# Picking rounds and modulation sums placed beside single attention jobs, the output product's wait split in four, and a square taken before the last output unit

## The reference

```python
mod = c_silu @ w_ada + b_ada                     # 1024 x 3072: the modulation
shift, scale, gate = split(mod, 3)
u = rms_norm(x, norm_g) * (1 + scale) + shift
z = u @ w_in                                     # 1024 x 8772, split by columns
# A: indexed attention: a query sees its top 64 keys by score
score = einsum('bth,bths->bts', iw * w_scale, relu(einsum('bthd,bsd->bths', iq, ik)))
top_val, top_idx = top_k(where(causal, score, -inf), 64)
# B: window attention with sinks; C: stick-breaking attention
merged = sigmoid(ma)*(ya @ w_br_a) + sigmoid(mb)*(yb @ w_br_b) + sigmoid(mc)*(yc @ w_br_c)
x = x + gate * (merged @ w_out)
```

## Time and profile before

| | |
|---|---|
| time, median of three runs | 1428.66 us |
| the profiled execution's own time | 1429.06 us |
| its span, first to last instruction | 1427.3 us |
| PE busy | 1371.8 us, 96% |
| DVE busy | 662.4 us, 46% |
| ACT busy | 419.9 us, 29% |
| POOL busy | 167.2 us, 12% |
| read from HBM | 222.62 MB, 157 GB/s over the span |

### The profile page before, as it was taken

The page is one execution under the profiler, slowest core; times in us unless marked ns, Lnnn a source line. Parts: engine busy times, 40 slices in busy tenths (PEclk is TensorE's granted clock), DMA queues, the critical chain, the costliest instruction groups (busy, mean ns, idle before and its releaser), DMA issues.

```text
span 1427.3 us, 19283 instructions
## 1 busy us (share of the span) xinstructions
PE 1371.8 (96%) x7590; PEld 1127.4 (79%) x7590; DVE 662.4 (46%) x1458; ACT 419.9 (29%) x773; POOL 167.2 (12%) x191
## 2 busy tenths in 40 slices
PE   6989999999998999999999999999999999999996
PEld 4878888888776888888888878877777788887764
DVE  1475334554238644324245331245493532467466
ACT  2312222311020222334322312342344422433442
POOL 0202200000011030000021100013140000243000
PEclk9999999999998999999999999999999999999999
DMA  9645555565433544444333332446322334432230
GB/s 385 248 154 209 209 177 206 188 252 224 176 135 136 211 155 177 148 160 148 121 142 120 118 118 98 151 169 225 126 89 92 116 128 146 168 119 89 89 148 30
DMA packets 31915, 224.93 MB, mean 158 GB/s; under 512 B 3920, under 2 KB 4048, under 8 KB 5072
## 3 DMA queue, kind: packets, MB, share of 16 engines
q1 hardware_dynamic: 31824, 223.68, 42.6%
HBM read 222.62 MB, written 1.05 MB: 157 GB/s over the span
## 4 chain that ended last, share of the span: by engine, by line
PE 85%; DVE 10%; issue 2%; ACT 2%; POOL 1%; DMA 0%; DVEq 0%; SPq 0%; ACTq 0%; POOLq 0%
PE event L1003 42%; PE event L994 9%; PE event L1147 5%; PE event L1213 5%; PE logits L1079 3%; PE mixed_out L1135 3%; PE turns L1098 3%; PE event L1240 2%; PE event L1172 1%; PE event L1177 1%; PE logits L970 1%; DVE region L1734 1%; PE event L1313 1%; DVE region L2200 1%; PE event L982 1%
## 5 line engine op out<-in xcount | busy, mean ns | idle before, releaser
L1003 PE MATMUL event<-u,ring 128*128 128x256 f32 x3072 | 685.2, 382 | 4.8 <-ACT u L1350 2.4
L1003 PEld LDWEIGHTS event<-u,ring 128*128 128x128 f32 x3072 | 578.7, 191 | 97.8 <-issue 18.6
L994 PE MATMUL event<-ring,u 128*128 128x256 f32 (+1 forms) x704 | 152.0, 373 | 0.0
L994 PEld LDWEIGHTS event<-ring,u 128*128 128x128 f32 x704 | 128.1, 191 | 21.9 <-issue 5.6
L2281 POOL TENSOR_TENSOR raw<-raw,tables 128x512 f32<-128x512 f32 (+1 forms) x28 | 44.6, 1593 | 723.8 <-DVE turned L1807 538.3
L1410 ACT ACTIVATE region<-event 128x512 f32<-128x512 f32 x72 | 43.0, 597 | 273.3 <-PE event L1003 273.0
L1446 ACT ACTIVATE S<-logits,stat 128x512 f32<-128x512 f32 (+2 forms) x160 | 83.9, 536 | 130.0 <-DVE stat L1846 120.7
L1213 PE MATMUL event<-region,ring 128*128 128x256 f32 x384 | 85.1, 380 | 4.6 <-DVE region L1989 4.6
L1213 PEld LDWEIGHTS event<-region,ring 128*128 128x128 f32 x384 | 72.2, 190 | 17.1 <-issue 7.8
L1147 PE MATMUL event<-region,ring 128*128 128x256 f32 x384 | 84.2, 380 | 0.0
L1147 PEld LDWEIGHTS event<-region,ring 128*128 128x128 f32 x384 | 72.7, 190 | 10.8 <-issue 1.0
(11 more groups left out here) (246 smaller groups left out, 1346.9 us busy)
## 6 DMA issues: line engine op xcount, KB each, us to landing
ring<-in_w SPq DMA_DIRECT2D x196, 1024.0 KB, 4.9
region<-in_quick SPq DMA_DIRECT2D x8, 1024.0 KB, 18.7
region<-in_rows SPq DMA_DIRECT2D x1, 1536.0 KB, 8.2
tables<-in_two SPq DMA_DIRECT2D x1, 1472.0 KB, 7.9
x<-in_x SPq DMA_DIRECT2D x1, 1024.0 KB, 7.1
u<-in_cond_rows SPq DMA_DIRECT2D x1, 1024.0 KB, 7.9
x<-in_ctx SPq DMA_DIRECT2D x1, 1024.0 KB, 8.8
out<-x SPq DMA_DIRECT2D x4, 256.0 KB, 2.2
```

What stands on the lines that cost most here:

```text
L994: ins = mm(bank[:, t * 256:t * 256 + width], mem.u[:, q, k, t * P:(t + 1) * P], wt[:, k * 256:k * 256 + width], start=k == 0, stop=k == KB ...
L1003: ins = mm(bank[:, j * 256:(j + 1) * 256], wt[:, k * 256 + j * P:k * 256 + j * P + P], mem.u[:, q, k, :], start=k == 0, stop=k == KB - 1)
```

## The change

The halves of the modulation are no longer strewn evenly. In `one0` every half of `v0` (now all 12 units, before 8) gets a place of its own directly behind the `logits` or the `turn` of a job, or behind a late projection or merge; `w1` and `w0` go in pairs of halves behind the `turn` of the four C jobs and behind the late units. In `one1` only four units (`w1`) are left, before eight. The picking rounds leave `dots` and go in fours behind the `logits` of the C jobs, jobs 3 to 6. `merged_ready` now counts pairs of merged blocks, and the first half of the first output unit waits for one pair at a time. A fifth `m` projection moves in front of the `mix` of job 9. At the end of `one1`, `sq h1` moves ahead of `out 3`. In SBUF the work tile of the picking becomes the mask tile itself.

```diff
+def halves_of_rows(units):
+    out = []
+    for tag, i in units:
+        out += [[("mvr", i, tag)], [("mvs", i, tag)]]
...
+def behind(s, item, items):
+    n = s.index(item) + 1
+    s[n:n] = items
+def picks_beside(s):
+    sticks = [n for n, job in enumerate(JOBS_ONE) if job.kind == "C"]
+    rounds = [("pick", qt, i) for qt in (0, 1) for i in range(TOPK // 8)]
+    share = len(rounds) // len(sticks)
+    for k, n in enumerate(sticks):
+        behind(s, ("logits", n), rounds[k * share:(k + 1) * share])
...
 def script_one0():
-    fill += [[proj("gate", 0, i)] for i in range(6)] + [[proj("m", 0, i)] for i in range(4)]
+    fill += [[proj("gate", 0, i)] for i in range(6)] + [[proj("m", 0, i)] for i in range(5)]
...
-    s = modulate_by_rows(s, heavy(s)[3:-5], units_of("w0", 4, 5) + units_of("w1", 0, 1, 2, 3) + units_of("v0", 0, 1, 2, 3))
+    spots = [(kind, n) for n in range(len(JOBS_ONE)) for kind in ("logits", "turn")]
+    spots += [proj("m", 0, i) for i in range(5, 12)] + [("merge", br, half) for br in range(3) for half in (0, 1)][:-1]
+    spots.sort(key=s.index)
+    both = halves_of_rows(units_of("v0", 0, 1, 2, 3, 4, 5))
+    for spot, half in zip(spots, both):
+        behind(s, spot, half)
+    one = halves_of_rows(units_of("w1", 0, 1, 2, 3) + units_of("w0", 4, 5))
+    for k, spot in enumerate([("turn", n) for n, job in enumerate(JOBS_ONE) if job.kind == "C"] + spots[len(both):]):
+        behind(s, spot, one[2 * k] + one[2 * k + 1])
+    picks_beside(s)
...
 def script_one1():
+    last = next(f for f in fill if ("out", 3, (0,)) in f)
+    for f in fill:
+        if ("sq", "h1") in f:
+            f.remove(("sq", "h1"))
+    last.insert(last.index(("out", 3, (0,))), ("sq", "h1"))
...
-    s = modulate_by_rows(s, at[3:13] + [a + 2 for a in at[14:22]], units_of("v0", 4, 5) + units_of("w1", 4, 5))
+    rows = halves_of_rows(units_of("w1", 4, 5))
+    for k, n in enumerate((1, 2, 7, 8)):
+        behind(s, ("logits", n), [i for half in rows[2 * k:2 * k + 2] for i in half])
+    picks_beside(s)
...
                 for j in halves:
                     for k in range(KB):
+                        if one and item[1] == j == 0 and k % 2 == 0:
+                            eng.wait_ge(sems["merged_ready"], w.at("merged_ready", k // 2 + 1))
...
-                        if (br, half, n) == (2, 1, 1):
+                        if br == 2:
                             ins.then_inc(sems["merged_ready"], 1)
...
             elif kind == "dots":
-                pick_keys(w, item[1])
+                score_keys(w, item[1])
+            elif kind == "pick":
+                pick_round(w, item[1], item[2])
```

More of the change, by code:

```diff
@@ L166, in modulate @@
     return out
[L169 to L176, removed]
+def halves_of_rows(units):
+    out = []
+    for tag, i in units:
+        out += [[("mvr", i, tag)], [("mvs", i, tag)]]
         own = [j for t, j in units if t == tag]
         if i == own[-1]:
[L179 to L186, removed]
-    return out
+            out[-1].append(("bias", tag, 2 * own[0], 2 * own[-1] + 2))
+    return out
+def behind(s, item, items):
[7 more added lines that the diff above has]
+        behind(s, ("logits", n), rounds[k * share:(k + 1) * share])
 def units_of(tag, *groups):
@@ L404, in __init__ @@
         n["finished"] = kinds.count("final")
-        n["dots_ready"] = n["relu_done"] = n["picked"] = kinds.count("dots")
-        n["gates_done"] = n["merged_ready"] = kinds.count("gates")
+        n["dots_ready"] = n["relu_done"] = kinds.count("dots")
+        n["picked"] = sum(i[0] == "pick" and i[2] == TOPK // 8 - 1 for i in script)
+        n["gates_done"] = kinds.count("gates")
+        n["merged_ready"] = KB // 2 * kinds.count("gates")
         n["branch_ready"] = 3 * kinds.count("gates")
@@ L1201, in body @@
                 bank = mem.bank[e % BANKS]
[L1202 to L1206, removed]
+                src = mem.merged if one else mem.of[q, 0]["y"]
                 if not one and item[1] == 0 and 0 in halves:
@@ L2181, in body, with keys_of, score_keys @@
                 eng.wait_ge(sems["x_scaled"], w.at("x_scaled", KB * n))
-    def pick_keys(w, qt):
-        o, K = mem.one, P * (qt + 1)
-        score, work, top = o["score"][:, 0:K], o["work"][:, 0:K], o["top"]
+    def keys_of(qt):
+        cols = slice(0, P) if qt == 0 else slice(P, P + T)
+        return mem.one["score"][:, cols], mem.one["pick"][:, cols], mem.one["top"]
+    def score_keys(w, qt):
+        K = P * (qt + 1)
+        score, _, _ = keys_of(qt)
         eng.wait_ge(sems["relu_done"], w.at("relu_done", qt + 1))
-        ts(mem.small[:, 0:4], o["bv"][:, qt, P:P + 4], W_SCALE, None, ALU.mult).then_inc(mine, 1)
+        ts(mem.small[:, 0:4], mem.one["bv"][:, qt, P:P + 4], W_SCALE, None, ALU.mult).then_inc(mine, 1)
         eng.wait_ge(mine, w.linked())
@@ L2194, in pick_keys, with pick_round @@
             eng.wait_ge(mine, w.linked())
-        for i in range(TOPK // 8):
-            eng.nop(nofuse=True)
-            eng.max(top, work if i else score).then_inc(mine, 1)
-            eng.wait_ge(mine, w.linked())
-            eng.nop(nofuse=True)
-            eng.match_replace(work, top, work if i else score, TAKEN).then_inc(mine, 1)
-            eng.wait_ge(mine, w.linked())
-        tt(work, work, score, ALU.not_equal).then_inc(mine, 1)
-        eng.wait_ge(mine, w.linked())
-        pick = o["pick"][:, 0:P] if qt == 0 else o["pick"][:, P:P + T]
-        stt(out=pick, in0=work, scalar=-NEG, in1=mem.t1["causal2"][qt], op0=ALU.mult, op1=ALU.add).then_inc(sems["picked"], 1)
-        eng.wait_ge(sems["picked"], w.at("picked", qt + 1))
+    def pick_round(w, qt, i):
+        score, pick, top = keys_of(qt)
+        eng.nop(nofuse=True)
+        eng.max(top, pick if i else score).then_inc(mine, 1)
+        eng.wait_ge(mine, w.linked())
+        eng.nop(nofuse=True)
+        eng.match_replace(pick, top, pick if i else score, TAKEN).then_inc(mine, 1)
+        eng.wait_ge(mine, w.linked())
+        if i == TOPK // 8 - 1:
+            tt(pick, pick, score, ALU.not_equal).then_inc(mine, 1)
+            eng.wait_ge(mine, w.linked())
+            stt(out=pick, in0=pick, scalar=-NEG, in1=mem.t1["causal2"][qt], op0=ALU.mult, op1=ALU.add).then_inc(sems["picked"], 1)
+            eng.wait_ge(sems["picked"], w.at("picked", qt + 1))
     eng.memset(mem.cond[:, :, :], 0.0).then_inc(sems["cond_zeroed"], 1)
```

16 lines of the change are left out of this document (7 added, 9 removed).

## The result

The changed kernel takes 1410.76 us, the median of four runs (1409.35 to 1411.23), against 1427.82 (1425.71 to 1429.28) for the kernel before: a ratio of 0.987, 95% interval 0.986 to 0.988. The forecast was 1411.9 us. The profiled execution took 1411.23 us and its span is 1409.5, 17.8 less than before.

A forecast was written before the change was run, and what follows sets the result against it. The prediction took PE, busy in 96% of the span, as the bound, with only idle and low-clock time to win. Gains of 21.2 us less 4.4 of ring waits gave 16.8, so 1411.9 us; range 1409 to 1415.

The forecast's parts named there:

- First wait: PE's 5.4 us wait before the logits of job 1 in `one0` shrinks to 0.8 us: 6.4 us saved, clock included.
- Second wait: PE's 6.7 us wait before the logits of job 0 in `one1`, put down to picking, goes: 9.0 us saved, clock included.
- Ring waits: In `one0`, late transfers make PE wait 2.3 us before `gate 1` and 2.1 before `gate 5`: 4.4 us cost.
- PE has six matmuls it may do (7.07 / 32 = 0.22 us each, 1.3 us): Before the first output products, PE's work during the last merge pair: 2.7 us saved in `one0`, 1.3 in `one1`.
- 0.2 to 0.5 us: The size of PE's waits forecast to remain before the two first output products.
- `m 4` and the closing: 1.2 us saved before the `mix` of job 9, and 0.6 us at the end of `one1`.
- DVE busy time is the same: Sign expected in the changed kernel's profile: DVE's total busy time does not change.
- (a): Rival, 22%: the ring in `one0` isn't late, so its 4.4 us cost is absent: 1407.5 us.
- (b): Rival, 17%: two ring waits in `one0` lower PE's clock, at a mean price of 2.3 us each: 1416.5 us.
- (c): Rival, 4%: VectorE becomes the bound of the C stage in `one0`, costing 34 us: 1446 us.
- (d): Rival, 4%: the rounds' microseconds come back at the next `turn` or `mix`; only 6 us gained: 1422.7 us.

The follow-up runs named there:

- experiment 1: The kernel before with only the picking rounds moved behind the logits of jobs 3 to 6: 1410.29 us, ratio 0.989.
- experiment 2: The changed kernel with each layer's sixteen picking rounds back behind the scores, ahead of all jobs: 1415.23 us, ratio 0.991.
- experiment 3: The changed kernel with both halves of four two-condition units in `one0` behind the `turn`, one-condition sums behind the rounds: 1405.00 us, repeated 1405.78.
- experiment 8: The changed kernel with every MAX and MATCH_REPLACE of a picking round issued twice: 1423.57 us, ratio 0.997.
- experiment 6: The changed kernel with `m 4` back behind the `mix` of job 9 and `sq h1` back behind the last output unit: 1413.11 us (one run).
- experiment 9: The changed kernel with the modulation sums strewn as in the kernel before, all else as changed: 1405.72 us, ratio 0.984.
- experiment 7: The changed kernel, unaltered, profiled once more: 1408.35 us (one run).

## Why the forecast held, step by step

**First wait: right.** The forecast took 6.4 us off. The logits of job 1 start 4.76 us earlier, and behind them 0.94 + 0.89 us of low clock are gone (2.08 to 1.14, 8.06 to 7.17): 6.6. The gap left is 0.69 us (0.8 forecast). No slow clock follows it.

**Second wait: right in size, incomplete in cause.** 9.15 us instead of 9.0. The prediction put the wait down to the picking, and had the rotation behind the first tile's rounds and part of the second's. In `one1` it stands behind all sixteen and behind four sums. Experiments 1 and 2 say that DVE had these two loads ahead of the rotation, and that taking away either ends the wait or leaves 0.76 us of it. In `one0`, where only one half of a one-condition unit stood ahead, the rounds are the cause: with them back, 4.04 of the 5.43 us return.

**Ring waits: right.** 2.3 and 2.1 us were forecast before `gate 1` and `gate 5`, none elsewhere; they are 2.52 and 1.76. The chain to the first begins in DVE's timeline (columns as in the earlier trace rows):

```profile
157.94 0.96 DVE L1908 TENSOR_SCALAR PT<-logits 128x768 f32<-128x768 f32 x1
...
160.21 1.53 DVE L1751 CUSTOM_DVE_ANT_0 region<-ring,region 128x1024 f32<-128x1024 f32 x1
...
161.78 1.53 DVE L1751 CUSTOM_DVE_ANT_0 region<-ring,u 128x1024 f32<-128x1024 f32 x1
...
164.62 0.69 DVE L1809 COPY region<-event 128x512 f32<-128x512 f32 x1
165.41 0.43 DVE L2224 MAX8 small<-region 128x8 f32<-128x256 f32 x1
...
171.09 1.23 DVE L1751 CUSTOM_DVE_ANT_0 region<-ring,u 128x1024 f32<-128x1024 f32 x1
```

The queue's own timeline has the issue:

```profile
172.35 6.69 SPq L891 DMA_DIRECT2D ring<-in_w  x4
```

And PE's has `gate 1`:

```profile
177.27 3.07 PE L1022 MATMUL event<-u,ring 128*128 128x256 f32 x13 [2.52 <-DMA ring<-in_w]
```

The last sum ends at 172.3, the queue issues at 172.35, and the product starts 4.9 us later, the median of the earlier trace rows. For `gate 5` the last sum ends at 209.9 and the product starts at 214.78. Two of the sums take 1.53 instead of 1.23 us beside POOL, 0.6 us that the forecast took as nothing. Experiment 3 shows that the position of the unit makes these waits. The first needs the rounds (it is gone in experiment 2) and grows with them (experiment 8); the second has none in its chain and stays.

**The step that failed: "PE has six matmuls it may do (7.07 / 32 = 0.22 us each, 1.3 us)".** I divided by the 32 records of a unit, but counted the products in the code, of which each leaves two records. PE has 2.75 us of work on the first three pairs. In the changed kernel the last pair is ready before PE needs it, as the timeline of both engines shows; its DVE row answers to the earlier trace rows:

```profile
355.78 4.48 PE L1230 MATMUL event<-region,ring 128*128 128x256 f32 x20
356.05 0.69 DVE L2006 TENSOR_TENSOR region<-event,region 128x512 f32<-128x512 f32 x1 [1.30 <-PE event L1166]
356.78 0.69 DVE L2008 TENSOR_TENSOR region<-region 128x512 f32<-128x512 f32 x1
```

The addition ends at 357.5, and PE's thirteenth record is due at 355.8 + 2.6 = 358.4. So the waits of "0.2 to 0.5 us" aren't there, and this term gave some 0.6 us more than its 4.0.

**`m 4` and the closing: right.** 1.27 and 0.68 us by experiment 6, for 1.2 and 0.6. ACT's timeline at the closing, against the earlier trace rows, has the scan's square 7 us earlier, and only the norm's square ahead of the copies:

```profile
842.02 0.63 ACT L1501 ACTIVATE rs<-region 128x512 f32<-128x512 f32 x1
849.26 0.63 ACT L1494 ACTIVATE u<-x 128x512 f32<-128x512 f32 x1 [6.61 <-DVE x L2084]
849.92 1.23 ACT L1528 ACTIVATE region<-event 128x512 f32<-128x512 f32 x2
```

**The clock elsewhere: not in the sum.** The profile of before has 1.6 us of low clock at the closing of `one1` (its rest is 479.19 us; experiment 1, with the same waits there, takes 477.61 at the full clock). The profile of the changed kernel hasn't, but has 1.65 us in the second block. The two cancel. That the span's 17.8 us came within 1.0 of the forecast's 16.8 is luck in so far.

**"DVE busy time is the same": wrong by 7.3 us, less.** The sums are part of it: fewer of them meet POOL. The groups of sums by their tiles, with a mean of 1231 and 1263 ns in place of 1264 and 1303:

```profile
L1751 DVE CUSTOM_DVE_ANT_0 region<-ring,u 128x1024 f32<-128x1024 f32 x48 | 59.1, 1231 | 1.7
L1751 DVE CUSTOM_DVE_ANT_0 region<-ring,region 128x1024 f32<-128x1024 f32 x32 | 40.4, 1263 | 11.2 <-issue 5.0 <-DMA ring<-in_w 4.3 <-DVE mod_w L1751 1.0
```

That is 2.9 us. Most of the other 4.4 are in four groups of two to four instructions each, which lose about 1 us a group. One of them, a TENSOR_SCALAR of 128x4, took 1.12 us at 435.54 us of the kernel before, beside POOL's rotation, and 0.17 at 422.26 with POOL idle. That this holds for all of them isn't shown. Of the meetings with POOL, 0.86 us lay on PE's path, in the second wait (experiment 2).

**The rivals.** (a), the ring isn't late, is refuted: it is, by 4.3 us. It would have been true of experiments 1, 3 and 9. (b), the clock falls behind the ring waits, didn't come about at 2.5 and 1.8 us (four profiles of kernels with both waits), but did at 6.9. The rule of the Trainium skill, TensorE: Matmul & The Clock Gate, section HAM oscillation, was weighed there. It tells of waits for transfers of some 3 to 5 us; the trace agrees for the long one, and the gaps of 2.5 and 1.8 us are shorter than those that the page tells of. It was the prediction that carried the rule over to them, and there it did not hold. (c), VectorE becomes the bound, is refuted: no wait of PE in the C stage of `one0` is for VectorE, and 4.5 us more rounds a C job cost 12.8 us in all, not 36. There is not much room left, though: with them VectorE is busy for 17.30 of the 20 us in the row of experiment 8. The four rounds behind the logits of jobs 3 and 4 do run beside POOL in the changed kernel, and aren't stretched. POOL's timeline:

```profile
125.63 1.71 POOL L2308 TENSOR_TENSOR raw<-raw,tables 128x512 f32<-128x512 f32 x1 [53.29 <-DVE turned L1824]
```

DVE's, in the same two microseconds:

```profile
126.32 0.30 DVE L2224 MAX8 small<-region 128x8 f32<-128x128 f32 x1
...
126.80 0.28 DVE L2227 MATCH_REPLACE8 region<-small,region 128x128 f32<-128x128 f32 x1
```

0.30 and 0.28 us are their lengths without POOL too (one hand-over between two of them was 0.4 us longer). The Trainium skill, GPSIMD Engine Reference, section Key points, says that instructions of two SBUF inputs contend with GpSimd; the sums, of two inputs, did (1.53 and 2.18 us for 1.23), and the rounds, of one, didn't, so the trace agrees. (d), the gain is given back, is refuted by the table: no stretch of the first block became longer.

**What the change is worth by its parts.** The rounds give some 17 us (experiment 1; by the stretches 17.3, of which 1.6 is the clock at the closing). The split gives 2.5 + 1.9 (2.0 + 1.9 where it is taken out of the changed kernel), m 4 1.3 and `sq h1` 0.7. The new places of the sums cost 4.3 us in the rest of `one0` as the change has them (experiment 9 against it), and gain 0.5 where the halves of a unit stay together (experiment 3 against 9).

## What to carry to other kernels

Where a ring of buffers is refilled strictly in order, a unit that is freed late delays the unit that stands a ring's length behind it: count from that unit's place to the product that wants its successor, and keep long work out of the time between a unit's first and last use. Before you name the cause of a wait, add up all that stands ahead of it on the engine that is late; two loads can each be enough to remove. And run the largest part of a change by itself: here it alone gave the gain of the medians, and the rest held some 6.4 us of gain and 4.3 of cost.

## What was not expected of the hardware

**A slow clock behind a wait of about 2 us comes and goes.** All twelve profiles have a wait of 2.35 us at the start of `one1` and one of 2.1 to 2.45 us in the second block. A mean clock of 0.91 follows the first in five of them and the second in seven, and the same kernel had it now here, now there (experiment 7). It costs 0.9 to 1.2 us at the first place and 1.65 at the second. The length of the wait doesn't order them: a wait of 1.96 us in the prologue had the low clock behind it in all twelve (0.91 from 20 to 40 us), one of 1.55 us at the closing of `one1` in one of four, and the ones of 2.96 us before an output product and of 2.4 to 2.5 us before `gate 1` never. Waits of 0.7 us before logits had none behind them in any profile, those of 4.04 to 6.87 us had it always. What decides between is open; no experiment here tells it.

**The start of a run and the low clock move its time.** PE's first wait, for ACT in the prologue, is 8.2 to 10.4 us in twelve profiles. Two kernels were profiled twice. The changed kernel took 1411.23 and 1408.35 us, and 2.1 of the 2.9 us lie ahead of the first fixed place; the one of experiment 3 took 1402.21 and 1405.35, and there it is 0.8 of 3.1 us, while 2.5 are low clock behind the two waits named above. Where the clock was the same, the stretches behind the prologue repeated to 0.02 us, so a term of half a microsecond is measured there and not by the median.
